# A re-ordered last turn, and the first down products of two column pairs in alternation, in a hybrid decoder layer

## What is computed

```python
u = rmsnorm(x, norm_attn)
proj = u @ w_in                      # q, k, v, indexer, z, conv inputs, dt
att = att_fn(q, k, v, qi, wi, ki)    # 8 heads, each query sees its top 128 (130) keys
y, h_fin = ssd_scan(xs, dt, A, Bm, Cm, h0, chunk)   # 16 Mamba heads
y = rmsnorm(y.reshape(B, T, SSM_WIDTH) * jax.nn.silu(z), ssm_norm)
h = x + jnp.concatenate([att, y], axis=-1) @ w_out  # 2048 x 2048
f = rmsnorm(h, norm_ffn)
h = h + (jax.nn.silu(f @ w_gate) * (f @ w_up)) @ w_down   # hidden width 5632
```

## Time and profile before

| | us |
|---|---|
| median of 3 runs | 2797.06 |
| lowest and highest of them | 2794.60, 2797.34 |
| the profiled execution | 2797.83 |
| its span on the core | 2796.0 |
| PE busy in it | 2698.8 (97%) |
| DVE, ACT, POOL busy | 1797.4, 1034.1, 393.2 |

### The profile page before, as it was taken

The page is one execution under the profiler, slowest core; times in us unless marked ns, Lnnn a source line. Parts: engine busy times, 40 slices in busy tenths (PEclk is TensorE's granted clock), DMA queues, the critical chain, the costliest instruction groups (busy, mean ns, idle before and its releaser), DMA issues.

```text
span 2796.0 us, 49441 instructions
## 1 busy us (share of the span) xinstructions
PE 2698.8 (97%) x20313; PEld 2607.2 (93%) x20313; DVE 1797.4 (64%) x2593; ACT 1034.1 (37%) x1538; POOL 393.2 (14%) x166
## 2 busy tenths in 40 slices
PE   8999999999999879999999999999999999899997
PEld 7988999888888769989999999999999999899996
DVE  3333699566566562458777777777777777777423
ACT  5233222333333342344343434434333443533223
POOL 2322333222222113320000000000000000000231
PEclk9999999999999989999999999999999999999998
DMA  6322222666666663423334333333433554645521
GB/s 224 124 77 82 96 93 85 173 177 178 189 179 189 178 208 112 142 86 108 124 118 143 110 125 116 116 117 117 135 109 108 188 158 153 241 142 164 203 107 68
DMA packets 394992, 388.94 MB, mean 139 GB/s; under 512 B 25949, under 2 KB 355269, under 8 KB 391704
## 3 DMA queue, kind: packets, MB, share of 16 engines
q1 hardware_dynamic: 375976, 364.33, 41.4%
q10 hardware_dynamic: 18800, 21.58, 2.2%
HBM read 319.11 MB, written 68.00 MB: 138 GB/s over the span
## 4 chain that ended last, share of the span: by engine, by line
PE 70%; issue 13%; DVE 6%; POOL 5%; DMA 2%; SPq 2%; ACT 1%; ACTq 0%; POOLq 0%; DVEq 0%
PE PS L1452 44%; PE PS L946 14%; PE PS L1436 5%; POOL WL L830 4%; PE PS L1148 1%; DVE mt L2307 1%; DVE ex L2299 1%; SPq L553 1%; DVE WL L2465 1%; PE PS L1387 1%; PE PS L1188 0%; DMA WRAW<-in_w_out 0%; PE PS L1177 0%; DVE xo_t L2614 0%; PE PS L1344 0%
## 5 line engine op out<-in xcount | busy, mean ns | idle before, releaser
L1452 PE MATMUL PS<-xo_t,WH 128*128 128x288 f32 x2544 | 516.0, 297 | 14.4 <-DVE WL L2465 4.0
L946 PE MATMUL PS<-AH,WH 128*128 128x288 f32 (+1 forms) x2144 | 481.2, 306 | 6.6 <-POOL WL L860 2.6
L946 PE MATMUL PS<-AH,WL 128*128 128x288 f32 (+1 forms) x2144 | 462.1, 297 | 0.0
L946 PE MATMUL PS<-AL,WH 128*128 128x288 f32 (+1 forms) x2144 | 461.5, 297 | 0.0
L1452 PEld LDWEIGHTS PS<-xo_t,WH 128*128 128x128 f32 x2544 | 411.7, 190 | 16.1 <-issue 16.1
L1452 PE MATMUL PS<-xo_x,WH 128*128 128x288 f32 x1936 | 389.3, 295 | 2.3 <-DVE xo_x L2553 1.0
L946 PEld LDWEIGHTS PS<-AH,WH 128*128 128x128 f32 (+1 forms) x2144 | 345.9, 190 | 37.0 <-issue 34.9
L1452 PE MATMUL PS<-xo_t,WL 128*128 128x288 f32 x1272 | 377.1, 296 | 0.0
L946 PEld LDWEIGHTS PS<-AH,WL 128*128 128x128 f32 (+1 forms) x2144 | 347.8, 190 | 0.0
L946 PEld LDWEIGHTS PS<-AL,WH 128*128 128x128 f32 (+1 forms) x2144 | 347.5, 190 | 0.0
L2465 DVE TENSOR_TENSOR WL<-WRAW,WH 128x1024 fp32r<-128x1024 f32 x201 | 245.8, 1223 | 109.1 <-ACT WH L1884 107.9
(11 more groups left out here) (393 smaller groups left out, 3762.5 us busy)
## 6 DMA issues: line engine op xcount, KB each, us to landing
WRAW<-in_w_gate SPq DMA_DIRECT2D x22, 2048.0 KB
WRAW<-in_w_up SPq DMA_DIRECT2D x22, 2048.0 KB
WRAW<-in_w_down SPq DMA_DIRECT2D x32, 1024.0 KB
WRAW<-in_w_in SPq DMA_DIRECT2D x14, 2048.0 KB, 8.1
raw<-in_w_in SPq DMA_DIRECT2D x48, 512.0 KB, 4.6
vca<-in_cache_v SPq DMA_DIRECT2D x256, 64.0 KB, 2.7
WRAW<-in_w_out SPq DMA_DIRECT2D x16, 1024.0 KB, 8.0
kca<-in_cache_k SPq DMA_DIRECT2D x232, 64.0 KB, 2.0
```

Of the source, the lines that this page charges most:

```text
L946: last = nc.tensor.matmul(G[gslot][0:width, h, 0:HALF], wt[:, half if slot is None else slot, k % 8, 0:width], act[:, k, h * HALF:(h + 1) ...
L1452: last = mm(out, wt[:, k, :], act[:, m, k, :], start=(j in (0, 1, 3) and k == 0 and wt is wh and m == 0), stop=(k == 7 and wt is wl), skip ...
```

## The change

In the last turn: the first half of `first` is requested at the end of turn 7, and with it blocks 0 and 1; blocks 2 to 5 stay in turn 8. The states of the last Mamba pair go to `h0x`, in the upper half of `AH` (blocks 8 and 9), which is not used any more by then. So they are loaded earlier, and the second half of `first` can be requested in turn 8, once turn 7's states are stored. ACT's work is put in another order (the evacuations of `xtok` and of two key blocks before the first weight cast and the decays; casts of blocks 0 to 3 together; weight casts `C3 + 1`, `C3 + 2` and `C3 + 4` each one place earlier). `mix_high(8)` now waits for the store of `h0x`. DVE makes the low parts of blocks 0 and 1 after four decay products. PE turns the last attention row after three steps of tile 1 instead of six. In all turns `sz` is now the last load of `load_mamba`.

In the feed-forward part: the products of q = 44 and 45, and of 52 and 53, alternate from the fourth on, so that the new operands are needed at places 0, 1, 2, 4, 6, 8 and 10 (`NEED`) instead of 0 to 6. The weights of q + 1 are requested behind the operand of j = 3, and partial results of q + 1 are kept in `kept2`. Nothing is added to or taken from the arithmetic.

```diff
@@ -179,0 +180 @@
+        h0x = sb("h0x", [P, NB, P], at=spot["AH"][0] + 8 * NT * 4)
@@ -202,0 +204 @@
+        kept2 = sb("kept2", [P, 3, HALF], at=spot["us2"][1])
@@ -378,0 +381,4 @@
+        NEED = (0, 1, 2, 4, 6, 8, 10)
+        for q in FIRST:
+            seq[7 * q:7 * q + 14] = [(q, 0), (q, 1), (q, 2), (q + 1, 0), (q, 3), (q + 1, 1), (q, 4), (q + 1, 2), (q, 5), (q + 1, 3), (q, 6),
+                                     (q + 1, 4), (q + 1, 5), (q + 1, 6)]
...
@@ -536,0 +542 @@
+                for e in range(2):
@@ -537,0 +544 @@
+                one(sp.dma_start(sz[:, :], rows(zS, i)))
...
@@ -572,2 +579,2 @@
-                    sp.wait_ge(s["mixa"], 16 * 6)
-                    load_mix(0, 0, 6)
+                    sp.wait_ge(mx_in[0], 16)
+                    load_mix(0, 2, 6)
@@ -576,2 +583 @@
-                    sp.wait_ge(s["w_lo"], C3)
-                    sp.dma_start(first[:, 0:8, :], wo_v[:, 0:8, 0:256]).then_inc(mx_in[2], 16)
+                    load_states(a)
@@ -583 +589 @@
-                if a > 0:
+                if a > 0 and units:
@@ -588,0 +595,2 @@
+                    sp.wait_ge(s["hout"], 16 * 7)
+                    sp.dma_start(first[:, 8:16, :], wo_v[:, 8:16, 0:256]).then_inc(w_ld[0], 32)
@@ -590 +598 @@
-                    sp.wait_ge(mx_in[0], 16)
+                    sp.wait_ge(mx_in[0], 32)
@@ -615,0 +624,2 @@
+                        sp.wait_ge(s["w_lo"], C3)
+                        sp.dma_start(first[:, 0:8, :], wo_v[:, 0:8, 0:256]).then_inc(mx_in[2], 16)
@@ -618,0 +629,2 @@
+                        sp.wait_ge(s["mixa"], 16 * 6)
+                        load_mix(0, 0, 2)
@@ -670,2 +681,0 @@
-            sp.wait_ge(s["hout"], 16 * 8)
-            sp.dma_start(first[:, 8:16, :], wo_v[:, 8:16, 0:256]).then_inc(w_ld[0], 32)
@@ -769,0 +780,2 @@
+                    if j == 3:
+                        load_weights(q + 1)
@@ -773 +784,0 @@
-                    load_weights(q + 1)
@@ -843 +853 @@
-            act.wait_ge(s["w_used"], c - 1)
+            act.wait_ge(s["w_used"], c - (2 if isinstance(c, int) and c == C3 + 4 else 1))
...
+            return kept2 if q - 1 in FIRST else kept
...
@@ -1348 +1362 @@
-                    for k in range(6):
+                    for k in range(3):
@@ -1351 +1365,2 @@
-                    out_step(1, 6)
+                    for k in range(3, 7):
+                        out_step(1, k)
@@ -1712,4 +1727,2 @@
-                elif j == 6:
-                    act.wait_ge(mx_in[0], 32)
-                elif j < 6:
-                    act.wait_ge(mx_in[0], 16)
+                elif j < 7:
+                    act.wait_ge(mx_in[0], 16 if j < 2 else 32 if j < 6 else 48)
@@ -1716,0 +1730,2 @@
+                    if j == 8:
+                        act.wait_ge(s["hout"], 16 * 8)
...
+                def decays():
...
+                    act.wait_ge(s["ssm_in"], LOADS * i)
...
+                if units:
+                    decays()
@@ -1745,0 +1766,3 @@
+                if not units:
+                    hi_p(C3, 0, 0, 0)
+                    decays()
@@ -1753,4 +1775,0 @@
-                else:
-                    mix_high(0)
-                    mix_high(1)
-                    hi_p(C3, 0, 0, 0)
@@ -1765,2 +1784,2 @@
-                    mix_high(2)
-                    mix_high(3)
+                    for j in range(4):
+                        mix_high(j)
@@ -1784,0 +1804,2 @@
+                if not units:
+                    hi_p(C3 + 1, 2, 0, 1)
@@ -1825 +1846,2 @@
-                    hi_p(C3 + 1, 2, 0, 1)
+                    act.wait_ge(s["lg_done"], 5 * 7 + 5)
+                    hi_p(C3 + 2, ATT_FIRST[2], 0, 3)
@@ -1851,2 +1872,0 @@
-            act.wait_ge(s["lg_done"], 5 * 7 + 5)
-            hi_p(C3 + 2, ATT_FIRST[2], 0, 3)
@@ -1856,0 +1877 @@
+            hi_p(C3 + 4, 0, 1)
@@ -1890 +1911,5 @@
-                if q:
+                if q == FIRST[0] + 1:
+                    act.wait_ge(s["t_st"], 16 * 16)
+                elif q == FIRST[1] + 1:
+                    act.wait_ge(s["e_add"], ADD[FIRST[0] + 1, 6])
+                elif q:
@@ -1892 +1917 @@
-                copy(kept[:, n, :], F[up][:, BANK[j], 0:HALF]).then_inc(s["e_cp"], 1)
+                copy(kept_in(q)[:, n, :], F[up][:, BANK[j], 0:HALF]).then_inc(s["e_cp"], 1)
@@ -1909 +1934 @@
-                if c >= 4:
+                if c >= 5:
@@ -1949,2 +1974,2 @@
-                j = n + 4
-                if 0 <= j < 7:
+                if n + 4 in NEED:
+                    j = NEED.index(n + 4)
@@ -2358,3 +2382,0 @@
-                else:
-                    for j in range(2):
-                        mix_low(j)
@@ -2370,0 +2393,3 @@
+                if not units:
+                    for j in range(2):
+                        mix_low(j)
...
```

More of the change, by code:

```diff
@@ L532, in load_mamba @@
                 sp.dma_start(cf[:, :], rows(xcS, i // 4 + 10)).then_inc(s["bc_in"], 16)
-                one(sp.dma_start(sz[:, :], rows(zS, i)))
                 for e in range(2):
@@ L536, in load_mamba @@
                     one(sp.dma_start(abc[:, e, :], bass.AP(acS.tensor, i * (2 * NT) + e * NT, [[0, P], [1, NT]])))
+                for e in range(2):
                     one(sp.dma_start(dcol[e * DS:(e + 1) * DS, :], bass.AP(I["d_skip"].tensor, i * 2 + e, [[0, DS], [1, 1]])))
+                one(sp.dma_start(sz[:, :], rows(zS, i)))
             def load_states(i):
-                sp.dma_start(h0[:, :, :], bass.AP(I["state_ssm"].tensor, i * (P * P), [[P, P], [NM * DS * P, NB], [1, P]])).then_inc(s["h0_in"], 16)
+                sp.dma_start((h0x if i == 7 else h0)[:, :, :], bass.AP(I["state_ssm"].tensor, i * (P * P), [[P, P], [NM * DS * P, NB], [1, P]])).then_inc(s["h0_in"], 16)
             def store_states(i):
                 sp.wait_ge(s["h_done"], 2 * i)
-                sp.dma_start(bass.AP(O["ssm_sample"].tensor, (i - 1) * (P * P), [[P, P], [NM * DS * P, NB], [1, P]]), h0[:, :, :]).then_inc(s["hout"], 16)
+                sp.dma_start(bass.AP(O["ssm_sample"].tensor, (i - 1) * (P * P), [[P, P], [NM * DS * P, NB], [1, P]]), (h0x if i == 8 else h0)[:, :, :]).then_inc(s["hout"], 16)
             def load_k(a, b, rows, i=None):
@@ L932, in cached_keys_t, with kept_in @@
             return kcaT[:, c, :] if c < 2 else pt[:, c - 2, :]
+        def kept_in(q):
+            return kept2 if q - 1 in FIRST else kept
         def mixed(j):
@@ L1168, in state_t @@
                 for b in range(4):
-                    last = tr(bank(f"hTb{g}")[:, b * P:(b + 1) * P], h0[:, 4 * g + b, :], ident[:, :])
+                    last = tr(bank(f"hTb{g}")[:, b * P:(b + 1) * P], (h0x if i == 8 else h0)[:, 4 * g + b, :], ident[:, :])
                 tmade(last, f"hTb{g}")
@@ L1733, in turn_act @@
                     hi3(i, 2)
-                act.wait_ge(s["ssm_in"], LOADS * i)
-                actv(ea[:, :], ea[:, :], ACT.Exp).then_inc(s["ea_done"], 1)
-                for e in range(2):
-                    ins = actv(elt[:, e, :].rearrange("p (c j) -> p c j", j=1), abc[:, e, 0:NP].rearrange("p (c j) -> p c j", j=P)[:, :, P - 1:P], ACT.Exp)
-                    ins.then_inc(s["ea_done"], 1)
+                def decays():
+                    act.wait_ge(s["ssm_in"], LOADS * i)
+                    actv(ea[:, :], ea[:, :], ACT.Exp).then_inc(s["ea_done"], 1)
+                    for e in range(2):
+                        ins = actv(elt[:, e, :].rearrange("p (c j) -> p c j", j=1), abc[:, e, 0:NP].rearrange("p (c j) -> p c j", j=P)[:, :, P - 1:P], ACT.Exp)
+                        ins.then_inc(s["ea_done"], 1)
+                if units:
+                    decays()
                 if later:
@@ L2415, in turn_dve @@
                     nc.vector.memset(ones[:, :], 1.0).then_inc(s["h_init"], 1)
+                hs = h0x if i == 8 else h0
                 for g in range(2):
@@ L2418, in turn_dve @@
                     for b in range(4):
-                        ins = stt(h0[:, 4 * g + b, :], h0[:, 4 * g + b, :], els[:, 4 * g + b:4 * g + b + 1], bank(f"us{g}")[:, b * P:(b + 1) * P], ALU.mult, ALU.add)
+                        ins = stt(hs[:, 4 * g + b, :], hs[:, 4 * g + b, :], els[:, 4 * g + b:4 * g + b + 1], bank(f"us{g}")[:, b * P:(b + 1) * P], ALU.mult, ALU.add)
                     ttaken(ins, f"us{g}")
@@ L2526, in gather @@
                 dve.wait_ge(s["p_done"], POS[q, j] + 1)
-                kept_in = None if n is None else KEEP[q, (0, 2, 3)[n]]
+                kept_at = None if n is None else KEEP[q, (0, 2, 3)[n]]
                 if q >= NPAIR:
@@ L2532, in gather @@
                         parts_added[0] += 1
-                        dve.wait_ge(s["e_cp"], kept_in)
-                        tt(dst, dst, kept[:, n, :], ALU.add).then_inc(s["e_part"], 1)
+                        dve.wait_ge(s["e_cp"], kept_at)
+                        tt(dst, dst, kept_in(q)[:, n, :], ALU.add).then_inc(s["e_part"], 1)
                         dve.wait_ge(s["e_part"], parts_added[0])
```

## The result

| | before | after |
|---|---|---|
| median of the runs, us | 2797.20 | 2781.15 |
| lowest and highest, us | 2794.60, 2797.38 | 2776.42, 2782.55 |
| the profiled execution, us | 2797.83 | 2782.55 |
| its span, us | 2796.0 | 2779.7 |

The ratio after to before is 0.9942, with a 95% interval from 0.9925 to 0.9959: 16 us less, where 24 were forecast. Timed again beside the last experiments it is 0.9941 (0.9928 to 0.9955). So the time is inside the range, and a third of the gain is missing.

What follows compares the result with a forecast made beforehand. PE sets the pace, but DVE limits the two openings and ACT's order delays PE in the last turn. 2797.8 less 18 (last turn) and 6 (openings) gave 2773.8, predicted as 2773 us; range 2768 to 2787.

Steps and rivals of the forecast that it cites:

- Rival C: Openings: TensorE stays at its lower clock through them, 2816 us; chance 0.04.
- E: No effect: PE's chain in the last turn is closed elsewhere, by DVE; 2796 us, chance 0.03.
- The last turn, first half: Last turn: waits for `xtok` and `ktok` leave PE's way, key transposes start 8.8 us earlier, tile 1 at 1012.8.
- the terms taken at nothing: Last turn: block 6 late 0 to 2 us, POOL's `C3`, `C3+1` splits 0 to 1.4 us each; taken 0.
- rival A: Last turn: a DMA (decays, block 6, values, `h0x` store) comes late, half of the 18 us left, 2783; chance 0.15.
- the forecast's own walk: Last turn: `xtok` out at 971.3, decay loads land 973.4, `ktok` by 977.3, key transposes start then, not 986.11.
- The second half: Last turn, tile 1 to tile 2: tile 2 at 1036.2 without a wait; the whole last turn gains 18 us.
- Block 9's place: Last turn: block 9 ready at about 1024.2, before 1036.6, its low part delayed beside POOL's split.
- 15 steps, 12 us: Last turn, from block 9 on: PE has 15 steps, 12 us, to 1036.2, and tile 2 follows at once.
- The openings: Feed-forward openings, set by DVE's queue: gain 3.9 us in the first and 3.2 in the second, 7.1 together.
- 1.1 for the clock: Openings: 1.1 us taken off the 7.1 for PE's clock, leaving 6 us.
- the list of moved requests: Openings: `t3` there ten us before ACT reaches it; weights of q = 46 up to 12 us an opening, taken 0.

Runs made afterwards that it cites:

- the combination: The change plus own `dcol`/`sz` semaphore, early `C3+1` cast, blocks 9, 10 cast earlier, `C3+3` low part on DVE, pair 44 sums earlier: 2773.5 us.
- the last one: The combination with the cast of block 6 moved behind two decay exponentials: 2774.1 us, ratio 0.9917 to before.

## Why the prediction was right or wrong

**Right.** What bounds the kernel, and that both parts act through it: the two waits for ACT's order went, block 9 is the last long wait, tile 2 starts without one at full clock, DVE stays the busiest engine in the openings (42.4 and 42.2 of 45 us). Rival C did not happen (0.89 and 0.96 in the openings), nor E.

**The last turn, first half: 8.8 us forecast, 6.2 measured** (58.0 in the mean of the two readings before, 51.8 in the mean of six). What failed are the terms taken at nothing, which is rival A's mechanism, at a part of its price. By the forecast's own walk the key transposes start 14.1 us behind `attS`; they start at 14.4 to 15.3, since ACT waits 0.45 to 1.41 us for the decay loads. The first output step was to come about 8 us earlier and came 6.6 earlier (26.0 and 19.4 us behind `attS` in the means). Behind it nothing was gained: 32.4 us against 32.0 before, with block 6 late by 0.7 to 2.0 us and POOL's split of `C3 + 1` holding DVE for up to 2.1. PE's matmuls as a whole were no slower than before: 39.9 to 42.9 us of busy time for the 300, 41.5 in the mean, against 40.5 and 42.7 in the old order.

That these terms make up the whole difference is argued, not shown. With each of them removed, alone or together, tile 1 came no earlier than 51.5 us. Two things stand in the way of that test. In the three kernels with `C3 + 1` right behind `C3` (alone, in the combination and in the last one) the split holds DVE at a worse place, and the first output step comes at 20.6 us. And in those three the matmuls behind that step were slow: 29.3 to 29.6 us of busy time at a clock of 0.87 or 0.88, with 2.1 us of waits, where the repeat of the change took 26.2 us at 1.00, with 4.9 us of waits. But this clock differs by itself: for that part the six readings of the change's order have 0.89, 0.90, 0.90, 0.90, 0.95 and 1.00. So whether a removed wait lowers it, or each execution has its own, stays open.

**The second half: 9.2 forecast, 6.7 measured** (5.9 and the 0.8 of tile 2's start, which in the one trace that the forecast had was 1.6). Block 9's place was right to 0.4 us: 11.4 us behind tile 1's start forecast, 11.8 measured, POOL's collision included. What failed is "15 steps, 12 us": they took 13.8, as 4 us of slow matmuls follow the wait of 3.47 us. That is the step of the forecast that failed here. The windows of after ahead of that wait, across it and behind it have a clock of 1.00, 0.79 and 1.00:

```profile
1017.00:1025.00 8.00, 8.00 (x61) 7.86 (x60) 6.53 (x10) 2.23 (x4) 0.00 (x0) 1.00 1.00 323
1025.00:1033.00 8.00, 4.44 (x21) 4.05 (x21) 7.01 (x8) 3.54 (x6) 2.34 (x1) 0.79 0.75 255
1033.00:1042.00 9.00, 9.00 (x70) 9.00 (x69) 4.39 (x7) 3.65 (x5) 2.40 (x1) 1.00 0.38 124
```

Such a wait was read from the earlier trace rows for tile 2, and priced there at 1.6 us, but not for block 9, where the forecast itself left PE idle for some 3 us until 1024.2.

**The openings: 7.1 us less 1.1 for the clock forecast, 3.4 measured.** The first: 3.9 forecast, 1.2 measured, 2.7 with the sums moved. The step that failed is the list of moved requests. It priced operands and weights, and left out the sums of pair 44 behind them. They were issued at 2227.3 and landed 8.9 us later, and DVE stood ready 6.6 us after the request; before, the request was at 2241.8 and DVE's first add at 2251.8, 10 us later. The second: 3.2 forecast, 2.25 measured. Here the walk of DVE's queue took no gap, while DVE waits four times, 0.3 to 0.8 us, for a cast on ACT, 1.9 us in all; before it had 2.4 us of such waits in as long a stretch. The discount for the clock was not needed: the sixth product of the first opening ran slow (5.8 us instead of 3.2) without a change of the stretch: in the repeat that product took 4.8 us and the stretch was 191.2 us instead of 190.9. Of the signs that the forecast named, PE's waits stayed below 2 us in the second opening (1.33 at most behind the marked one) and not in the first (3.42).

**The sum.** 12.9 + 3.4 = 16.3 us by the markers, and 16 by the timing. The measured time lies inside the range, 8 us above the point forecast: nearly every term erred to the same side. Only the discount of 1.1 us for the clock went the other way; it was put on for a reason that did not come true and covered a part of the late sums, which is luck.

The rule cited from the Trainium skill (SBUF — State Buffer, Who interferes with whom) served the forecast of block 9, and moving that split to DVE took the stretch from tile 1 to tile 2 from 24.7 to 22.0 us. The same section says that copies and tensor-scalar operations can also contend. That was not used, and the traces have cases of both: 1.56 instead of 0.17 us for the copy of `els`, 2.56 instead of 0.47 for two decay differences.

## What to carry to other kernels

When a wait is taken out, what stood behind it moves forward and meets the next load or split; price that, and don't take it at nothing because the engines have gaps elsewhere. Price also the matmuls behind every wait that remains. Take the same stretch from several executions before a difference of 2 us is explained: the same code had 50.1 to 52.7 us. When requests are moved forward, list everything that is queued behind them, small loads too. A split that POOL makes beside a DVE that sets the pace can cost DVE most of the split's length; if DVE can do it itself in less (1.23 against 2.1 us), give it to DVE.
